# Seven block products in place of eight in the up projection of one MLP, on one Trainium2 core

## The reference

```python
hn = rms_norm_3(h, norm_mlp_w[layer])
h = h + jnp.square(jax.nn.relu(hn @ w_up[layer])) @ w_down[layer]
out = rms_norm_3(h, norm_final_w)
```

## Time and profile before

| | us |
|---|---|
| median of 3 runs (lowest, highest) | 3664.6 (3659.71, 3666.09) |
| the profiled execution, its own time | 3661.55 |
| its span | 3659.4 |
| PE, DVE, ACT busy in the span | 3598.4, 2144.2, 1579.6 |

### The profile page before, as it was taken

How to read it: one execution, slowest core, us unless ns; L and a number is a source line. 1 busy time by engine, 2 the same in 40 slices (tenths; PEclk the granted TensorE clock), 3 DMA queues, 4 the chain that set the end, 5 groups by cost and what they waited for, 6 DMA issues and landing times.

```text
span 3659.4 us, 50653 instructions
## 1 busy us (share of the span) xinstructions
PE 3598.4 (98%) x21121; PEld 2959.4 (81%) x21121; DVE 2144.2 (59%) x3262; ACT 1579.6 (43%) x2544; POOL 81.4 (2%) x85
## 2 busy tenths in 40 slices
PE   8999899999999999999999999999999999999998
PEld 5888778788888878888888889888888888888887
DVE  5741687775345578757588564366655266555333
ACT  5451666644334444535344452333443333434333
POOL 0000121000000000000000000000000000000000
PEclk9999899999999999999999999999999999999999
DMA  5124321324322222222222322222222222223222
GB/s 202 47 72 113 78 68 51 119 92 115 106 97 98 96 84 78 96 97 93 90 78 93 98 88 91 93 81 87 86 94 97 93 87 81 84 95 121 98 98 87
DMA packets 118891, 340.27 MB, mean 93 GB/s; under 512 B 20089, under 2 KB 32393, under 8 KB 118537
## 3 DMA queue, kind: packets, MB, share of 16 engines
q1 hardware_dynamic: 116424, 331.52, 28.0%
q0 software_dynamic: 2240, 5.51, 0.7%
HBM read 318.47 MB, written 20.06 MB: 93 GB/s over the span
## 4 chain that ended last, share of the span: by engine, by line
PE 94%; DVE 4%; ACT 1%; issue 1%; DMA 0%; SPq 0%; ACTq 0%; DVEq 0%
PE ps L341 54%; PE ps L319 28%; PE ps L1337 1%; PE ps L821 1%; PE ps L2847 1%; PE ps L1045 1%; PE ps L1693 1%; PE ps L1660 1%; DVE n_s L1782 1%; PE ps L1348 1%; PE ps L2276 0%; DVE g_D L1524 0%; PE ps L2303 0%; PE ps L1670 0%; PE ps L1380 0%
## 5 line engine op out<-in xcount | busy, mean ns | idle before, releaser
L341 PE MATMUL ps<-acts,w_hi 128*128 128x512 f32 (+1 forms) x6064 | 1813.1, 383 | 2.5 <-ACT l_vf L2683 0.8
L341 PEld LDWEIGHTS ps<-acts,w_hi 128*128 128x128 f32 x6064 | 1110.2, 188 | 231.9 <-issue 10.6
L341 PE MATMUL ps<-acts,w_lo 128*128 128x512 f32 (+1 forms) x3032 | 1136.1, 381 | 0.0
L280 DVE TENSOR_TENSOR w_lo<-w_raw,w_hi 128x1024 fp32r<-128x1024 f32 x539 | 657.8, 1221 | 390.9 <-ACT w_hi L275 387.9
L275 ACT ACTIVATE w_hi<-w_raw 128x1024 fp32r<-128x1024 f32 x539 | 563.6, 1050 | 500.3 <-DMA w_raw<-in_w_mlp 316.5
L341 PEld LDWEIGHTS ps<-acts,w_lo 128*128 128x128 f32 x3032 | 561.5, 188 | 110.0
L319 PE MATMUL ps<-h_hi,w_hi 128*128 128x512 f32 x1528 | 478.0, 394 | 0.0
L319 PE MATMUL ps<-h_lo,w_hi 128*128 128x512 f32 x1528 | 471.1, 390 | 0.0
L319 PE MATMUL ps<-h_hi,w_lo 128*128 128x512 f32 x1528 | 470.9, 389 | 0.0
L386 DVE TENSOR_TENSOR h_lo<-u_act,h_hi 128x512 fp32r<-128x512 f32 x192 | 132.8, 692 | 436.4 <-ACT u_act L376 435.9
L402 DVE TENSOR_TENSOR xT<-xT,ps 128x1024 f32<-128x1024 f32 x191 | 232.8, 1219 | 235.1 <-PE ps L319 234.4
(11 more groups left out here) (392 smaller groups left out, 2944.0 us busy)
## 6 DMA issues: line engine op xcount, KB each, us to landing
w_raw<-in_w_mlp SPq DMA_DIRECT2D x384, 512.0 KB, 3.4
...
```

The lines of the kernel that those rows point to most:

```text
L280: nc.vector.tensor_tensor(w_lo[u.z][:, :], w_raw[u.z][:, :], w_hi[u.z][:, :].bitcast(F32), ALU.subtract).then_inc(w_split[u.z], 1)
L341: last = nc.tensor.matmul(ps[:, bank, 0:t1 - t0], w[:, k * P:(k + 1) * P], acts(h, low, k, t0, t1), start=(i_k == 0 and i == 0), stop=(i_k ...
```

## The change

In `mlp3[1]`, group 0 keeps its four up units. In groups 1 to 7 the ups go in pairs, `ua` and `ub`, 14 pairs in all. A pair is a product of a 2x2 block matrix of weights (`a11`, `a12` the two halves of the first unit, `a21`, `a22` of the second) with a 2x2 block matrix of activations (input channels by 256-token quarters). It is made with seven products of 4 blocks in place of eight, in the order first, fifth, second, sixth, third, fourth, seventh; each is 12 matmuls of 256 columns (`pair_pe`). First, sixth and seventh add up in one PSUM region (`grown`), which ACT copies out after each (`pair_act`: `m1_sum`, `u_act`, `m7_sum`) before PE may add the next.

VectorE forms three sums of weight blocks and one in place (`sums_dve`) and once, inside the norm, four folded activations (`fold_tokens_dve`, two calls of four instructions); each sum is split into high and low again (`split_pair_act`, `split_sums_dve`, and the segment `folded`, beside steps 0 to 3). DVE puts the outputs together in five additions on 256 columns (`pair_dve`). There is a fifth weight slot and a sixth place for hidden chunks in this stage. The order is now: ups 0 to 3, pair (1,0), four downs, pair (1,1), pair (2,0), four downs, and so on to pair (7,1), four downs. A pair (g,0) of groups 2 to 7 follows a pair directly; its preparation is written inside the pair before it (`inside`, `nxt`). Pair (1,0) and all (g,1) are prepared by `walk` two units ahead. Semaphores are those of earlier stages under new names (in the rows below `gg` is `pair_mm`, `gg_act` `pair_copied`, `gg_sum` `pair_relu`, `go_sq`, `go_sum` and `go_ln` those of the folded activations, `go_rs`, `go_norm` and `go_end` those of the sums; `na_comb` says that the fifth slot is split).

```diff
+        quarters = Region(out_at + (w_at - out_at) % PHASE, end)
+        t_low = Region(quarters.at, end).take("t_low", [P, 4, KQ, Q], F32R)
+        t_raw = quarters.take("t_raw", [P, 4, KQ, Q])
+        t_high = quarters.take("t_high", [P, 4, KQ, Q], F32R)
+        pairs_at = Region(half_at[0] + 4 * META, half_at[1])
...
             k = used[u.pool]
-            used[u.pool] += 1
+            used[u.pool] += u.kind != "ua"
...
+        def squares_low_dve(dve, u):
+            dve.wait_ge(hid_hi, u.chunk + 1)
+            nc.vector.tensor_tensor(hidden(1, u.chunk), as_hidden(u_act[:, u.chunk % 2, :], u.chunk), hidden(0, u.chunk).bitcast(F32),
+                                    ALU.subtract).then_inc(hid_ready, 1)
...
+        def pair_regions(b):
+            z = 6 + b.pair % 2
+            return ps[:, b.bank, 0:Q], ps[:, b.bank + 1, 0:Q], ps[:, b.bank + 1, Q:HALF], ps[:, z, 0:Q], ps[:, z, Q:HALF]
...
+            def product(out, weights, moving, start=True, stop=True):
+                for k in range(KQ):
+                    for i, (w, low) in enumerate([(weights[0], 0), (weights[0], 1), (weights[1], 0)]):
+                        last = nc.tensor.matmul(out, w[:, k * P:(k + 1) * P], moving(low, k), start=start and k == 0 and i == 0,
+                                                stop=k == KQ - 1 and i == 2,
+                                                skip_group_check=not (start and stop))
+                return last
...
+            if b.use:
+                pe.wait_ge(bank_free(b), b.use)
+            weights_split(pe, a)
+            product(grown, weights(a, 0), tokens_of(0, 0), stop=False).then_inc(pair_mm, 1)
+            pe.wait_ge(s_split, s_split0 + p + 1)
+            if p == 0:
+                pe.wait_ge(t_split, t_split0 + 4)
+            product(fifth, summed(0), folded(0))
+            product(second, weights(a, 1), tokens_of(1, 0)).then_inc(mm_done[a.z], 1)
+            pe.wait_ge(pair_copied, copied0 + 3 * p + 1)
+            product(grown, summed(1), folded(1), False, False).then_inc(pair_mm, 1)
+            product(third, summed(2), tokens_of(1, 1))
+            weights_split(pe, b)
+            product(fourth, weights(b, 1), folded(3)).then_inc(pair_mm, 1)
+            pe.wait_ge(pair_copied, copied0 + 3 * p + 2)
+            product(grown, weights(b, 0), folded(2), False).then_inc(mm_done[b.z], 1)
+
+        def pair_act(act, b):
+
+            a, p = b.mate, b.pair
+            grown = pair_regions(b)[0]
+            if b.nxt is not None:
+                split_act(act, b.nxt.mate)
+            act.wait_ge(pair_mm, mm0 + 3 * p + 1)
+            nc.scalar.activation(m1_sum, grown, ACT.Copy).then_inc(pair_copied, 1)
+            if b.nxt is not None:
+                split_pair_act(act, b.nxt)
+            act.wait_ge(pair_mm, mm0 + 3 * p + 2)
+            act.wait_ge(hid_ready, a.chunk - 1)
+            nc.scalar.activation(u_act[:, 0, Q:HALF], grown, ACT.Copy).then_inc(pair_copied, 1)
+            act.wait_ge(pair_out, out0 + 4 * p + 3)
+            relu_act(act, a)
+            unit_done(act, b)
+            nc.scalar.activation(m7_sum, grown, ACT.Copy).then_inc(pair_copied, 1)
+            act.wait_ge(pair_relu, relu0 + 2 * p + 1)
+            squares_act(act, a)
+            own_free(act, b)
+            relu_act(act, b)
+            act.wait_ge(pair_relu, relu0 + 2 * p + 2)
+            squares_act(act, b)
+
+        def relu_act(act, u):
+            t = u_act[:, u.chunk % 2, :]
+            bias = param("b1", 4 * u.gr + u.j) if u.bias else 0.0
+            nc.scalar.activation(t, t, ACT.Relu, bias=bias).then_inc(pair_relu, 1)
+
+        def pair_dve(dve, b):
+
+            a, p = b.mate, b.pair
+            grown, fifth, second, third, fourth = pair_regions(b)
+            if b.nxt is not None:
+                sums_dve(dve, b.nxt)
+                split_dve(dve, b.nxt.mate)
+            unit_done(dve, a)
+            dve.wait_ge(pair_copied, copied0 + 3 * p + 1)
+            dve.wait_ge(hid_ready, a.chunk - 1)
+            nc.vector.tensor_tensor(u_act[:, 0, 0:Q], m1_sum, second, ALU.add).then_inc(pair_out, 1)
+            if b.nxt is not None:
+                split_sums_dve(dve, b.nxt)
+            dve.wait_ge(pair_copied, copied0 + 3 * p + 2)
+            nc.vector.tensor_tensor(u_act[:, 0, Q:HALF], u_act[:, 0, Q:HALF], fifth, ALU.add).then_inc(pair_out, 1)
+            dve.wait_ge(pair_mm, mm0 + 3 * p + 3)
+            dve.wait_ge(pair_out, out0 + 4 * p + 2)
+            nc.vector.tensor_tensor(u_act[:, 0, Q:HALF], u_act[:, 0, Q:HALF], third, ALU.add).then_inc(pair_out, 1)
+            if b.nxt is not None:
+                split_dve(dve, b.nxt)
+            dve.wait_ge(pair_copied, copied0 + 3 * p + 3)
+            dve.wait_ge(hid_ready, b.chunk - 1)
+            nc.vector.tensor_tensor(u_act[:, 1, Q:HALF], m7_sum, fifth, ALU.add).then_inc(pair_out, 1)
+            nc.vector.tensor_tensor(u_act[:, 1, 0:Q], m7_sum, fourth, ALU.add).then_inc(bank_free(b), 1)
+            squares_low_dve(dve, a)
+            squares_low_dve(dve, b)
...
+        def sums_dve(dve, b):
+
+            a, p = b.mate, b.pair
+            s = s_raw[p % 2]
+            if p < 2:
+                unit_done(dve, before_seven[0])
+            else:
+                unit_done(dve, pairs[p - 2])
+            for u in (a, b):
+                dve.wait_ge(w_landed[u.z], landed_old[u.z] + 16 * u.turn + 16)
+            a11, a12 = (w_raw[a.z][:, i * HALF:(i + 1) * HALF] for i in range(2))
+            a21, a22 = (w_raw[b.z][:, i * HALF:(i + 1) * HALF] for i in range(2))
+            nc.vector.tensor_tensor(s[:, 0, :], a21, a22, ALU.add).then_inc(s_made, 1)
+            dve.wait_ge(s_made, s_made0 + 4 * p + 1)
+            nc.vector.tensor_tensor(a21, a11, a21, ALU.subtract).then_inc(s_made, 1)
+            nc.vector.tensor_tensor(s[:, 1, :], s[:, 0, :], a11, ALU.subtract).then_inc(s_made, 1)
+            dve.wait_ge(s_made, s_made0 + 4 * p + 3)
+            nc.vector.tensor_tensor(s[:, 2, :], a12, s[:, 1, :], ALU.subtract).then_inc(s_made, 1)
+            dve.wait_ge(s_made, s_made0 + 4 * p + 4)
+
+        def split_pair_act(act, b):
+            p = b.pair
+            act.wait_ge(s_made, s_made0 + 4 * p + 2)
+            split_act(act, b)
+            act.wait_ge(s_made, s_made0 + 4 * p + 4)
+            nc.scalar.activation(s_high[p % 2][:, :, :], s_raw[p % 2][:, :, :], ACT.Copy).then_inc(s_hi, 1)
+
+        def split_sums_dve(dve, b):
+            p = b.pair
+            dve.wait_ge(s_hi, s_hi0 + p + 1)
+            nc.vector.tensor_tensor(s_low[p % 2][:, :, :], s_raw[p % 2][:, :, :], s_high[p % 2][:, :, :].bitcast(F32), ALU.subtract)\
+                .then_inc(s_split, 1)
...
+        def prepare_dve(dve, u):
+            if u.kind == "ua" and not u.inside:
+                sums_dve(dve, u.pair_end)
+                split_dve(dve, u)
...
                     low(4)
+                    if m is rms_mlp3[1]:
+                        fold_tokens_dve(m, 0)
+                        dve.wait_ge(t_made, t_made0 + 4)
...
+                    if m is rms_mlp3[1]:
+                        fold_tokens_dve(m, 1)
...
+        def fold_tokens_dve(m, i):
+
+            one, other = m.q[:, 2 * i:2 * i + 2, :], m.q[:, (4 + 2 * i) % 6:(4 + 2 * i) % 6 + 2, :]
+            b11, b12, b21, b22 = one[:, :, 0:Q], one[:, :, Q:HALF], other[:, :, 0:Q], other[:, :, Q:HALF]
+            t = [t_raw[:, j, 2 * i:2 * i + 2, :] for j in range(4)]
+            m.wait(nc.vector, "scaled", 6 + 2 * i)
+            nc.vector.tensor_tensor(t[0], b12, b11, ALU.subtract).then_inc(t_made, 1)
+            nc.vector.tensor_tensor(t[2], b22, b12, ALU.subtract).then_inc(t_made, 1)
+            nc.vector.wait_ge(t_made, t_made0 + 4 * i + 1)
+            nc.vector.tensor_tensor(t[1], b22, t[0], ALU.subtract).then_inc(t_made, 1)
+            nc.vector.wait_ge(t_made, t_made0 + 4 * i + 3)
+            nc.vector.tensor_tensor(t[3], b21, t[1], ALU.subtract).then_inc(t_made, 1)
+
+        T_STEPS = 4
+
+        def folded_act(act):
+            act.wait_ge(t_made, t_made0 + 8)
+            for i in range(T_STEPS):
+                nc.scalar.activation(t_high[:, i, :, :], t_raw[:, i, :, :], ACT.Copy).then_inc(t_hi, 1)
+                yield
+
+        def folded_dve(dve):
+            for i in range(T_STEPS):
+                dve.wait_ge(t_hi, t_hi0 + i + 1)
+                nc.vector.tensor_tensor(t_low[:, i, :, :], t_raw[:, i, :, :], t_high[:, i, :, :].bitcast(F32), ALU.subtract)\
+                    .then_inc(t_split, 1)
+                yield
+
         def gla_pool(pool):
 
             pool.wait_ge(sa["end"], sa0["end"] + 2 * HB)
@@ -3082,6 +3345,35 @@
                         up(gr + 1, j)
             return us
...
+            def pair(gr, i, inside):
+                a, b = up("ua", gr, 2 * i), up("ub", gr, 2 * i + 1)
+                a.inside = b.inside = inside
+                a.pair_end, b.mate, b.pair, b.nxt = b, a, len(pairs), None
```

(26 more changed lines are left out.)

131 lines of the change are left out of this document (109 added, 22 removed).

## The result

The changed kernel takes 3675.3 us (median of 6 runs, 3674.3 to 3678.5) where the kernel before takes 3664.9 in the same series (6 runs, 3659.7 to 3666.1): a ratio of 1.0033, 95% interval 1.0021 to 1.0045, which is some 12 us; the two medians lie 10.4 us apart. The interval holds no 1, so the kernel is slower, if only by a third of a per cent. The forecast was 3673, in a range of 3662 to 3684.

The account below looks back on a forecast made before the run. PE was taken to bound the kernel, busy 98% of the span; -15.2 + 3.7 + 8.1 + 9.7 + 0.3 + 1.7 = +8.3 us gave a median of 3673 us, range 3662 to 3684.

Parts of the forecast that it names:

- Saving: In the 14 pairs on PE: a pair takes 9.79 us in place of 10.88, 15.2 us saved in all (11.2 to 19.1).
- The line through 264 and 512 columns: Pace of PE's matmuls: a slope of 0.430 ns per column through two traced shapes puts 256 columns at 116.6 ns.
- The rival of a lower rate: Pair matmuls on PE: 256 columns take 110.1 ns, 22.8 us are saved, median 3667, no change; chance 0.10.
- Wait 1: Up 1 of the stage: PE waits 3.7 us for DVE's addition behind the last down, delayed by the first folding call.
- Wait 2: Ahead of pair (1,0): the sum for half 0's final norm waits 8.1 us for its parts from DVE.
- Both waits count: Head of the stage: DVE's chain to the final norm's sum hangs on up 1's end, so 3.7 and 8.1 us add.
- Wait 3: Pairs (g,0) of groups 2 to 7: the sixth product waits 1.6 us for ACT's `m1_sum` copy, six times, 9.7 us.
- Wait 4: Group 7's downs behind pair (7,1): the fourth hidden chunk's low part comes 0.3 us late.
- Clock: After the idle stretch of 8 us the granted clock falls to half once, costing 1.7 us (0 to 3.4).
- The rival of a fall at each wait 3: Pairs (g,0) of groups 2 to 7: the clock falls each time, 6 x 1.7 us more, 3683, slower; chance 0.12.
- Costed at nothing: Second copy and `s_low` in pairs (g,1), weight loads, added DVE and ACT work, down units: no cost expected.
- Sum: Whole kernel: all terms together give +8.3 us, the profiled execution's 3661.6 becomes 3669.9, the median 3673.

## Why the prediction was right, and where its sizes were off

- **What bounds the kernel:** right. All of the time came from PE's own pace and from PE's waits.
- **Saving:** the term was too large, 15.2 for 11.2. The line through 264 and 512 columns fails at 256: 120.0 ns, the upper end of the range given. It is not that a floor holds 264 columns (the floor is at 112 ns): the curve jumps between 248 and 256. The rival of a lower rate, 110.1 ns, is out by the same rows.
- **Wait 1:** 3.7 forecast, 3.56 measured. The folding calls took 2.66 and 2.54 us for 2.7 and 2.55; the restart took 0.06 for 0.17.
- **Wait 2:** 8.1 forecast, 8.0 measured, with the chain through DVE in the order given. "Both waits count" holds in the account of this kernel: DVE's chain starts when ACT has worked off up 1. Whether they add as savings is open. With wait 1 cut by 2.5 us wait 2 grew by 1.5, but that edit also ended the folding, with which ACT's own chain starts, 2.3 us later.
- **Wait 3:** six times, at the sixth product, on ACT, with DVE not last: right. The size was 1.3 for 1.6 each. ACT's chain took 5.49 us for 5.63, the three products 4.32 for 4.20, which follows from the slower pace, and PE was back 0.05 us after the copy.
- **Wait 4:** 0.1 for 0.3. The low part came 4.05 us behind the pair's end, for 4.3.
- **Clock:** 3.6 for 1.7. The fall at wait 2 came as forecast and cost 2.1. It fell twice, and the reasoning that a fall behind wait 1 changes little failed: it cost 1.55 us beside wait 1, since up 1's end is what the rest hung on. The rival of a fall at each wait 3 is out: the clock is 1.00 there.
- **Costed at nothing:** held in every trace; the second copy, `s_low` and the loads never stood in PE's waits, except where a norm was moved beside them.
- **Sum:** +8.3 forecast, +12.2 in the stage: 4.0 from the pace, 1.9 from the clock, less 1.8 at wait 3. The median is only 2.3 over the forecast, and a part of that is luck. The forecast carried the 3.05 us over by which the profiled execution of before lay under its median; that of after lies 1.0 under its own. And wait 3's size erred against the pace and the clock. The mechanism was right at each place; the two terms that were mis-sized most are the saving (15.2 for 11.2) and the clock (1.7 for 3.6).
